# Expert turns ranked by load, six of them in packed column tiles, and ten key buffers for the decode attention

## The reference, cut to what matters

```python
def moe_ffn(x, w_router, wg, wu, wd):
    B, T, D = x.shape
    xf = x.reshape(B * T, D)
    logits = (xf @ w_router).astype(jnp.float32)
    top_v, top_i = lax.top_k(logits, TOP_K_EXPERTS)
    top_w = jax.nn.softmax(top_v, axis=-1)
    combine = jnp.sum(jax.nn.one_hot(top_i, N_EXPERTS, dtype=jnp.float32) * top_w[..., None], axis=1)
    out = jnp.zeros_like(xf)
    for e in range(N_EXPERTS):
        out = out + combine[:, e:e + 1].astype(x.dtype) * swiglu(xf, wg[e], wu[e], wd[e])
    return out.reshape(B, T, D)
...
def nsa_attend(q, g, q_pos, kc, vc, ks, vs, kw, vw, kw_pos, rel_bias):
...
    s_s = jnp.einsum('bqkgd,bkqmd->bkgqm', q, k_sel).astype(f32) + b_s
    p_s = masked_softmax(s_s, (pos_sel <= q_pos[:, None])[:, :, None])
    o_s = jnp.einsum('bkgqm,bkqmd->bqkgd', p_s.astype(v_sel.dtype), v_sel)
...
    s_w = jnp.einsum('bqkgd,bskd->bkgqs', q, kw).astype(f32) + bias_2d(rel_bias, q_pos, kw_pos)
```

## Time and profile before

| | us |
|---|---|
| Time, median of 3 runs | 2042.74 (2039.84 to 2043.71) |
| The profiled execution, its own time | 2039.63 |
| Its span, first to last instruction | 2037.8 |
| Decode, from its first block scores to the output projection | 817.71 to 990.79 |
| Eight expert turns on PE | 1066.98 to 2011.1 |

### The profile page before, as it was taken

One profiled execution on the slowest core, in us unless ns is written; L12 is line 12 of the kernel. 1 busy time (PEld: TensorE's weight loads), 2 busy tenths in 40 slices (PEclk: granted clock), 3 DMA queues, 4 the chain that ended last, 5 costly groups with the idle time before them and its releaser, 6 DMA issues.

```text
span 2037.8 us, 36628 instructions
## 1 busy us (share of the span) xinstructions
PE 1880.5 (92%) x15695; PEld 1519.6 (75%) x15695; DVE 373.8 (18%) x823; ACT 249.8 (12%) x539; POOL 138.1 (7%) x198
## 2 busy tenths in 40 slices
PE   6699998999999999767869999999999999999994
PEld 5489996777777776545659789695978869596982
DVE  2798011100003035434120000000000000000002
ACT  1001011100000135434120000000000000000001
POOL 2052000300000010332010000000000000000001
PEclk9799999899999989888879999999999999999997
DMA  9845556764654433687638999897989989798994
GB/s 240 222 144 178 182 168 218 296 221 144 244 182 132 118 147 122 217 267 241 154 110 271 303 292 314 277 327 262 345 298 299 311 279 322 266 345 278 320 308 152
DMA packets 354325, 484.74 MB, mean 238 GB/s; under 512 B 32612, under 2 KB 311150, under 8 KB 353580
## 3 DMA queue, kind: packets, MB, share of 16 engines
q1 hardware_dynamic: 325600, 392.40, 60.5%
q10 hardware_dynamic: 15500, 45.66, 6.8%
q0 software_dynamic: 13120, 45.15, 6.3%
HBM read 450.51 MB, written 40.98 MB: 241 GB/s over the span
## 4 chain that ended last, share of the span: by engine, by line
issue 48%; PE 42%; DMA 4%; ACT 2%; DVE 2%; another core or an unknown queue 1%; ACTq 1%; POOL 0%; SPq 0%; POOLq 0%; DVEq 0%
PE ps L1397 15%; PE ps L1427 8%; PE ps L1521 4%; DMA arena<-in_state_win_kv 3%; PE ps L1543 2%; PE ps L1566 2%; PE ps L1627 1%; PE ps L1708 1%; PE ps L1365 1%; PE ps L1772 1%; PE ps L1623 1%; ACT arena L870 1%; PE ps L1658 1%; PE ps L1640 0%
## 5 line engine op out<-in xcount | busy, mean ns | idle before, releaser
L1857 PEld LDWEIGHTS ps<-arena 128*128 128x128 f32 x5632 | 631.9, 192 | 5.3 <-issue 5.0
L1857 PE MATMUL ps<-arena 128*128 128x128 f32 x5632 | 632.4, 275 | 1.3 <-ACT arena L905 1.3
L1397 PE MATMUL ps<-arena 128*128 128x288 f32 x1216 | 303.4, 413 | 24.1 <-DMA arena<-in_conv_w_pw 19.0
L1867 PE MATMUL ps<-arena 128*128 128x512 f32 x704 | 304.2, 593 | 1.7 <-DVE arena L1309 1.7
L1397 PEld LDWEIGHTS ps<-arena 128*128 128x128 f32 x1216 | 235.0, 194 | 91.9 <-DMA arena<-in_conv_w_pw 19.5
L1867 PEld LDWEIGHTS ps<-arena 128*128 128x128 f32 x704 | 133.1, 190 | 168.1 <-issue 168.1
L1309 DVE TENSOR_TENSOR arena<-arena,ps 128x256 f32<-128x256 f32 x88 | 37.1, 421 | 882.0 <-ACT arena L921 882.0
L1427 PE MATMUL ps<-arena 64*64 64x128 f32 x4096 | 159.2, 310 | 3.8 <-issue 3.7
L1427 PEld LDWEIGHTS ps<-arena 64*64 64x64 f32 x4096 | 154.7, 249 | 8.1 <-issue 7.6
L1013 DVE SCALAR_TENSOR_TENSOR arena<-arena 128x256 f32<-128x256 f32 x240 | 120.1, 586 | 0.0
L921 ACT ACTIVATE arena<-ps 128x256 f32<-128x256 f32 x88 | 33.7, 383 | 531.5 <-PE ps L1857 531.4
(11 more groups left out here) (308 smaller groups left out, 1053.3 us busy)
## 6 DMA issues: line engine op xcount, KB each, us to landing
arena<-in_moe_w_gate SPq DMA_DIRECT2D x88, 1024.0 KB, 6.5
arena<-in_moe_w_up SPq DMA_DIRECT2D x88, 1024.0 KB, 7.2
arena<-in_moe_w_down SPq DMA_DIRECT2D x88, 1024.0 KB, 4.9
arena<-in_cache_kv SPq DMA_DIRECT2D x176, 256.0 KB, 5.4
arena<-in_cache_kv POOLq DMA_DIRECT2D x80, 256.0 KB, 7.0
xg_scratch<-arena POOLq DMA_DIRECT2D x26, 512.0 KB, 18.3
arena<-in_conv_w_pw SPq DMA_DIRECT2D x12, 1024.0 KB, 14.8
arena<-in_cmp_w ACTq DMA_DIRECT2D x6, 2048.0 KB, 22.9
```

Of the source, the lines that this page charges most:

```text
L1397: ins = mm(dst, w[:, k, c * P:(c + 1) * P], rhs[:, k, :], start=(k == 0), stop=(k == KD - 1))
L1857: ins = mm(dst, w[:, k, c * P:(c + 1) * P], XeT[:, k, :], start=(k == 0), stop=(k == KD - 1))
L1867: ins = mm(ps[:, 4 + c, :], He[:, 2 * k + kk, :], w[:, kk, 512 * c:512 * (c + 1)], start=(k == 0 and kk == 0), stop=(k == 10 and kk == 1))
```

## The change

**Ranking.** DVE sorts the experts by their number of rows (`rank8`). Turn 0 and 1 take the two largest and have room for 128 rows (`CAP` + 32), the other six 96 (`CAP`); what doesn't fit goes to the later passes as before. `orderI` holds which expert runs in which turn; SP waits for it (`rid_ready` at 2) and reads the expert's number at the head of each turn.

**Turns.** The first two turns run `experts` as before. The other six run `fewer`: the rows of the expert are three groups of 32 that stay stationary, and the weights move, 128 columns at a time (256 for down). Four such products, each in its own 32 columns of the array, fill the four 32-partition quarters of a PSUM bank. A unit is three runs of 32 products: gate for the first 64 rows, gate and up for the last 32, up for the first 64. So the gate slot is released after the second run. The hidden rows come out row by row and not column by column, so two transposes per unit (`columns_out`) and an ACT copy (`columns_in`) follow one unit later. ACT stores the results in three transfers instead of one.

**Decode.** Ten key slots (`key_slot`) instead of five, and the turned keys go back into the slot that they came from. All ten units of the first pair are loaded during the attention of the prompt. A unit of a later pair waits for the scores of the same unit one pair before (`s_unit`). The first two units of the next pair are turned ahead of this pair's softmax. ACT's copies follow that order. The scratch for the results is cleared in six more small pieces (`YZERO`).

```diff
+CAP = P - 32
+YZERO = 22 * 16
...
+        def key_slot(pr, u):
+            if pr == 0:
+                return (7 * 1024, KRING, KRING + 1024, KRING + 2048, 8 * 1024, KRING + 3072, KRING + 4096,
+                        9 * 1024, 0, 1024)[u]
+            if u < 2:
+                return QT0 + u * 1024
+            if u < 5:
+                return KV0 + (u - 2) * 1024
+            return KRING + (u - 5) * 1024
...
-            if 10 * pr + u >= 5:
-                eng.wait_ge(sem("kt_tr"), 10 * pr + u - 4)
+            if pr == 0:
+                eng.wait_ge(sem("pco_mm"), 1)
+            elif pr == 1 and u < 5:
+                eng.wait_ge(sem("prompt_done"), 1)
+            elif pr == 1:
+                eng.wait_ge(sem("s_unit"), (1, 2, 2, 3, 4)[u - 5])
             else:
-                eng.wait_ge(sem("pco_mm"), 1)
-            if u < 2 and pr == 1:
-                eng.wait_ge(sem("prompt_done"), 1)
-            elif u < 2 and pr > 1:
+                eng.wait_ge(sem("s_unit"), 5 * (pr - 1) + kt + 1)
+            if u < 2 and pr > 1:
                 eng.wait_ge(sem("o_mm"), pr - 1)
...
-            def experts(e, turn):
-
+            def experts(j, turn):
+                e = sp.value_load(orderI[0:1, bass.ds(j, 1)], min_val=0, max_val=NE - 1)
...
+            sp.wait_ge(sem("rid_ready"), 2)
             with sp.Fori(0, NE, 1) as e:
                 experts(e, e)
...
+                for u in range(11):
+                    if u:
+                        columns_in(u - 1)
+                    act.wait_ge(slot_used, turn * EPAD + (M0 + 2 * u + 2))
+                    act.wait_ge(sem("gu_ev"), turn * 11 + (u + 1))
+                    sc.activation(ee[:, u % 2, 0, :], ps[:, 2 + u % 2, 0:P], ACT.Silu)
+                    sc.activation(ee[64:, u % 2, 1, :], ps[0:64, 2 + u % 2, 2 * P:3 * P], ACT.Silu).then_inc(sem("gu_exp"), 1)
...
+                def columns_out(u):
+                    pe.wait_ge(sem("gu_ev"), turn * 11 + (u + 3))
+                    if u:
+                        pe.wait_ge(sem("ht_ev"), n * 11 + u)
+                    tr(ps[:, 7, 0:P], Hs[:, u % 2, 0, :], ident)
+                    tr(ps[:, 7, P:2 * CAP], Hs[64:, u % 2, 1, :], ident[64:, 64:]).then_inc(sem("ht_mm"), 1)
...
+                    for k in range(KD):
+                        for j in range(4):
+                            g, h = divmod(j, 2)
+                            mm(ps[quarter(j), bk, 0:P], XeT[:, k, quarter(g)], gate[:, k, h * P:(h + 1) * P], start=(k == 0),
+                               stop=(k == KD - 1), skip_group_check=True)
+                    if u:
+                        columns_out(u - 1)
...
+                    for kk in range(2):
+                        for g in range(3):
+                            for j in range(4):
+                                ins = mm(ps[quarter(j), 4 + g, 0:256], HT[:, k, 64 * g + 32 * kk:64 * g + 32 * kk + 32],
+                                         w[:, kk, 256 * j:256 * (j + 1)], start=(k == 0 and kk == 0), stop=(k == 10 and kk == 1),
+                                         skip_group_check=True)
...
                 if pr < PAIRS - 1:
                     block_scores(pr + 1)
+                    ktr(pr + 1, 0)
+                    ktr(pr + 1, 1)
+                    pe.wait_ge(sem("kt_out"), 10 * pr + 12)
...
-                if pr < PAIRS - 1:
-                    ktr(pr + 1, 0)
-                    ktr(pr + 1, 1)
```

More of the change, by code:

```diff
@@ L291, in build, with key_sem @@
         assert top_pa <= CB
+        def key_slot(pr, u):
[7 more added lines that the diff above has]
+            return KRING + (u - 5) * 1024
+        def key_sem(pr, u):
+            return f"kv_first{u % 2}" if pr == 0 else f"kv_in{u}"
+        assert KRING + 5 * 1024 == 7 * 1024 and 4 * KVC == 1024
         phase()
@@ L316, in build @@
         rkB = take(3, NE, NE)
+        HT = He.rearrange("p a b -> p (a b)")[:, 0:11 * 2 * CAP].rearrange("p (u c) -> p u c", u=11)
+        key8 = take(NE)
+        rank8 = take(NE)
+        place = take(2, NE)
+        cap8 = take(NE)
+        room8 = take(NE)
+        sort8 = take(NE, NE)
+        order8 = take(NE)
+        orderI = base0[0:1, cursor[0]:cursor[0] + NE].bitcast(I32)
+        cursor[0] += NE
         flag = base0[:, cursor[0]:cursor[0] + 1].bitcast(I32)
@@ L860, in _ @@
             for pr in range(PAIRS):
[L861 to L867, removed]
+                for g in range(10 * pr + (2 if pr else 0), min(10 * pr + 12, 10 * PAIRS)):
+                    act.wait_ge(sem("kt_tr"), g + 1)
+                    bk = 2 * (g % 2)
+                    sc.activation(view(key_slot(g // 10, g % 10), 2, 512), ps[:, bk:bk + 2, :], ACT.Copy)\
+                      .then_inc(sem("kt_out"), 1)
                 act.wait_ge(sem("s_max"), pr + 1)
@@ L1311, in experts, with fewer @@
                      .then_inc(sem("gu_ev"), 1)
-            with dve.Fori(0, NE, 1) as e:
-                experts(e, e)
+            def fewer(n, turn):
+                for u in range(11):
+                    x, w, bk = ee[:, u % 2], u % 2, 2 + u % 2
+                    dve.wait_ge(sem("gu_exp"), turn * 11 + (u + 1))
+                    if u >= 2:
+                        dve.wait_ge(sem("ht_mm"), n * 11 + (u - 1))
+                    v.tensor_tensor(Hs[:, w, 0, :], x[:, 0, :], ps[:, bk, P:2 * P], ALU.mult)
+                    v.tensor_tensor(Hs[64:, w, 1, :], x[64:, 1, :], ps[64:, bk, 2 * P:3 * P], ALU.mult)\
+                     .then_inc(sem("gu_ev"), 1)
+            with dve.Fori(0, 2, 1) as h:
+                experts(h, h)
+            with dve.Fori(0, NE - 2, 1) as s:
+                fewer(s, s + 2)
             dve.wait_ge(sem("flag_ready"), 1)
@@ L1841, in rows_in, with eslot @@
                 ins.then_inc(sem("xt_mm"), 1)
+            def eslot(turn, k):
+                s = k % RING
+                pe.wait_ge(full[s], turn * (16 * per[s]) + (counts[s] + 16 * (k // RING + 1)))
+                return ring[:, s, :]
             def experts(turn):
-                def eslot(k):
-                    s = k % RING
-                    pe.wait_ge(full[s], turn * (16 * per[s]) + (counts[s] + 16 * (k // RING + 1)))
-                    return ring[:, s, :]
                 pe.wait_ge(sem("xe_ev"), turn + 1)
@@ L1878, in _ @@
+            with pe.Fori(0, 2, 1) as h:
+                experts(h)
+            with pe.Fori(0, NE - 2, 1) as s:
+                fewer(s, s + 2)
             pe.wait_ge(sem("flag_ready"), 1)
```

146 lines of the change are left out of this document (108 added, 38 removed).

## The result

The changed kernel takes 2068.62 us (median of 4 runs, 2064.33 to 2070.5), the kernel before in the same session 2041.55. The ratio is 1.0128, with an interval from 1.0112 to 1.0145: 1.3% slower, where 1919 us was forecast. The profiled execution took 2064.33 us, its span is 2062.5.

What follows compares the result with a forecast made beforehand. PE bounds the expert turns, then the weights nearly equally; -95 (light turns) - 37 (decode) + 7 (start) + 1 (stores) = -124 us on 2039.63, span 1915.6, median forecast 1919 us. Range 1868 to 2005, some four fifths.

Steps and rivals of the forecast that it cites:

- What bounds the kernel: Expert turns: PE sets the pace at 117.86 us a turn; after the change the bound passes to the weights.
- The forecast's turn: Light expert turn: 102 us, between 97 and 110, limited by weights at 348 GB/s; gain 95 us over six turns.
- The light turn on PE, its products: Light turn: 27.4 to 29.0 ns a record, gate and up 57.9 to 61.2 us, down 28.9 to 30.6.
- that rival: Light turn: the array packs less well in long runs, 37.4 ns a record, turn 122, about 2040 us; chance 0.06.
- The transposes: Light turn on PE: 22 new transposes at 0.13 us each, 2.9 us a turn.
- Instructions: the step that failed: Light turn on PE: 21.4 instruction transfers at 0.16 us plus 2.0 for the jump, 5.4 us a turn.
- The rival: Light turns: instructions come too slowly through full DMA engines, up to 2.0 us a transfer; turn 136, 2123 us; chance 0.08.
- its point of decision: Instruction rival in light turns: decides from 1.4 us a transfer on, where a turn is 5 us longer than now.
- its rival: Turns full of short waits: the clock falls to 1.2 GHz, about 2420 us; chance 0.03 together with overflow.
- Decode: Decode: 29.5 us of key waits and 7 us of slow work go; -37 us, between -28 and -42.
- Start and stores: Before the first turn: 7 us for DVE's instructions and weights beside the scatter; last store in three pieces: 1 us.
- The sum: Whole kernel: -95 - 37 + 7 + 1 = -124 us, forecast 1919 us; chance 0.69.

Runs made afterwards that it cites:

- wide_flat: The wide kernel with PE's six light turns written out one after the other instead of a hardware loop; 1932.51 us, ratio 0.9464.
- thin_weights: The changed kernel with a quarter of the bytes loaded per weight slot in the six light turns, PE's instructions the same; 1915.2 us, ratio 0.9384.
- heavy_two: The decode_only kernel with PE's loop over eight long turns made four passes of two turns, some 3200 instructions; 2002.26 us, ratio 0.9795.
- decode_only: The kernel before with only the decode's part of the change, nothing of the experts; 2002.41 us, ratio 0.9805.
- ranked_heavy: The changed kernel with all eight turns the long ones of 128 rows; ranking, wait for the order and decode stay; 2011.45 us, ratio 0.9852.
- wide: The changed kernel with light-turn gate and up products moving 256 columns instead of 128, two units in three runs; 1956.8 us, ratio 0.9578.

## Why the prediction was wrong

**What bounds the kernel.** Right: PE set the pace of the turns, and a turn whose PE part is short is limited by the weights. In wide_flat they give a turn of 104.8 us at 341 GB/s, where the prediction said 102 at 348. The forecast's turn exists, but not in this kernel.

**The light turn on PE, its products.** Right. In thin_weights a run of 64 records takes 1.75 us (from 1381.58 to 1383.33), 27.4 ns a record (forecast 27.4 to 29.0); 33 runs are 57.8 us. Down is 28.9 a turn, as forecast. So the array packs four tiles in long runs as well as in the decode's bursts, and that rival fell; the 3.17 that the prediction estimated for four tiles from the Trainium skill (TensorE: Matmul & The Clock Gate, Part 3) is 224 / 55 = 4.1 here. The wait for DVE's product cost nothing, as forecast: none of PE's waits in the four turns is for it. The transposes were mis-sized: two take 0.46 us (from 1385.25 to 1385.71) and not 0.26, since each stands alone, 5.1 a turn against 2.9. With 1.1 for the rows and about 3 us at the lower clock behind the jump (41 records in 2.51 us, then 64 in 3.40) this is 95.9; 102.6 less 5.9 of waits is 96.7. Forecast 93.

**Instructions: the step that failed.** "I take 21.4 x 0.16 + 2.0 for the jump back to the head = 5.4, since code of the same density was fed there." The count was right (23 in the trace, with what the jump adds). The prices were not. The jump cost 9.7 us of waits and not 2.0; the rest cost 14.7 and not 21.4 x 0.16 = 3.4. Together this is 24.4 a turn, 1.1 a transfer. On top of it the products took 7.2 us a turn longer than in thin_weights, by the three lines of gate and up in equal numbers of turns, the changed kernel first, thin_weights second:

```profile
L1988 PE MATMUL ps<-arena 128*32 128x128 f32 x2812 | 101.3, 289 | 45.3 <-issue 45.2
L2002 PE MATMUL ps<-arena 128*32 128x128 f32 x2816 | 100.2, 292 | 33.5 <-issue 33.5
L1996 PE MATMUL ps<-arena 128*32 128x128 f32 x2816 | 95.0, 286 | 7.6 <-issue 7.5
```
```profile
L1992 PE MATMUL ps<-arena 128*32 128x128 f32 x2816 | 91.3, 281 | 23.4 <-issue 23.4
L2000 PE MATMUL ps<-arena 128*32 128x128 f32 x2816 | 90.4, 282 | 0.0
L2006 PE MATMUL ps<-arena 128*32 128x128 f32 x2816 | 85.9, 273 | 0.0
```

296.5 less 267.6 is 28.9 us in four turns, 7.2 a turn. Not all of it is the lower clock. A run that is cut pays its start twice: 0.82 + 1.51 = 2.33 us for the 64 records around 1291.84, where 64 in one piece took 1.95 just behind them. At 0.38 the 34 waits that the changed kernel has more in four turns (43 against 9) are, as an estimate, 3 us a turn, which leaves 4 for the clock. Waits and longer runs together, (24.4 - 5.9) + 7.2 = 25.7, are the distance of the two kernels' turns, 127.7 - 102.6 = 25.1, within 0.6 us.

The density was not the same, and the prediction's own rows said so: the compression takes 37.4 ns a record, 4.8 us for 256 instructions, the light turn 27.4, 3.5 us. Nor were the DMA engines: over the compression's stretch of the earlier trace rows the window shows 177 GB/s,

```profile
117.00:310.00 193.00, 186.87 (x4508) 175.39 (x4510) 85.44 (x136) 20.83 (x53) 45.01 (x62) 0.99 0.56 177
```

a share of 0.56, where the light turns were to fill them. The rival named both conditions, the full engines and the wait for a turn on them, and was right in its mechanism. Its price of 2.0 a transfer was too high (a turn of 136 against 127.7), but its point of decision, 1.4, was too high as well: it left out that stops bring the lower clock and cut runs in two, and that PE's own part is 3 to 4 us longer. It had 0.08 where nothing measured spoke against it: the one row that did came from other conditions.

The Trainium skill (Runtime: NRT & Kernel Launch, Instruction fetch mechanics) gives PE a memory of 2048 instructions that is refilled in blocks of 256, calls the crossing of a block mostly hidden, and warns of jumps. The blocks and the jump agree with the traces here (252 instructions and some register work between two stops; 5.2 to 5.7 us at each head). Hidden they are in thin_weights, wide_flat and heavy_two, but not in the changed kernel; there the measurement decides.

**The clock.** It fell, as its rival said, but to 0.92 on the mean, and only in stops and behind them.

**Decode.** Right: -37 was forecast; decode_only shows -37 to -39, the trace -41. Nothing else came late there: a pair takes 31.6 us, where 33 were left without the waits.

**Start and stores.** 7 and 1 were forecast, 9.0 is what ranked_heavy costs above decode_only: DVE 2.0 (forecast 2.2), the rest the scatter and the rows beside the weights.

**The sum.** -39 + 9 + 57 = 27 us, the measured 2068.62 - 2041.55. The pieces are differences of the same four times, so that they must add up; beside the forecast's -37 + 8 - 95 they show that the error is all in the light turns.

## What to carry to other kernels

Before a loop body on TensorE grows past what stays resident, divide its time by its instruction transfers: what matters is the time that 256 instructions last against the fetch of the next, on DMA engines as busy as they will be there. If it is short, use fewer and wider products, and write the loop out if its end is dense; the same packing, which had added 57 us, then took 79 off (wide_flat against ranked_heavy). A price for a resource that was measured in another stage holds only for that stage's pace and load.

## What the runs showed of the hardware

- A body of 1600 instructions ran without any transfer, one of 3200 was fetched again in each pass (15 transfers), and it cost nothing at 112 ns a record.
- A 16 KB instruction transfer takes 1.07 us on DMA engines at 0.32 and at 0.83 alike. What full engines add lies ahead of its start (2.3 us at the jump shown): 256 instructions in 3.5 us are too fast for it at a share of 0.83 to 0.90, not at 0.32; in 7 us they are slow enough at 0.97 to 1.01.
- The jump back of a loop too long to stay cost two waits behind products of 55 ns a record: 5.9 us together on engines at 0.32, 8.4 (wide) and 9.7 (the changed kernel) on full ones. Behind products of 432 ns, on engines at 0.93, it cost nothing.
- What stays open: on which engine or queue an instruction transfer waits, and how far ahead it is asked for; the traces show when it starts, not when it was asked for.
